# Moving one tile's routing ahead of the last output product in a one-core hybrid decoder layer

## The chip, the core and the metric

One Trainium2 chip, one of its cores, one launch of the kernel. The time is device microseconds (us) from start to end, the median of the runs shown. Below, PE is TensorE, DVE VectorE, ACT ScalarE, POOL GpSimd and SP SyncE, as in the profile.

## The reference

One decoder layer over 256 tokens of width 1024, float32.

```python
h = rmsnorm(x, g_mix)
proj = h @ w_in                      # columns for four token mixers A, B, C, D
b[i] = mixer_i(proj)                 # 256 wide each
merged = sum_i sigmoid(h @ w_gate[i]) * (b[i] @ w_br[i])
x = x + merged @ w_o
h2 = rmsnorm(x, g_ffn)
g_logits = h2 @ w_rg + b_rg          # 4 groups: the largest is taken
e_logits = h2 @ w_re + b_re          # 32 experts, 8 in each group: the two largest of that group
gate = p_group * softmax(the two)
y = sum over the two: gate * ((silu(h2 @ w1[e]) * (h2 @ w3[e])) @ w2[e])
out = rmsnorm(x + y, g_final)
```

## The kernel before

The tokens are two tiles of 128 rows (t = 0, 1), a row of 1024 is two halves of 512 (n = 0, 1). Each engine has a queue of its own, written out by hand in the order of the code; what crosses engines is a semaphore wait. Exact products of float32 weights are made in three PE passes over a high and a low part (`three`).

**The output product.** `out_product(t, n)` computes the quarter (t, n) of merged @ w_o: 8 slices k, three matmuls each, 24 in all. The order of the quarters on PE is (0,0), (1,0), (0,1), (1,1). `turn_tile(1, merged)` stands in the middle of the first; `turn_tile(0, x)`, eight transposes, in the middle of the last. When a quarter is done, DVE adds it to `x` (`add_product`), and `s["wo"]` counts quarters.

**Splitting and turning.** For the experts' gathers each row of x is split in three bf16 parts: `first_part`, `second_part` (ACT), `remain`, `third_part` (DVE), a quarter at a time. For the router the rows of a tile are turned (`turn_tile(t, x)`, PE), weighted by the norm's weights (`weighted_turned`, DVE, into `h2T`) and multiplied by the router's 36 columns (`route(t)` on PE).

**The choices.** When both tiles' router logits are there, DVE makes the choice of group and experts for both tiles at once, a chain in which every instruction waits for the one before (`link`): largest group logit, its one-hot, the mask of the other groups, largest expert, its one-hot, second largest. It ends in `asg`, the assignment. PE counts places from it (five small matmuls, `s["pos"]`), DVE makes `slot` and the one-hot `pick` of the first pair, and PE gathers the rows of the first two experts with `pick` (48 matmuls; L1737). Meanwhile PE puts x into the banks where results are summed (`absorb`) and makes 20 small matmuls whose result is not used (L1720).

**The experts.** 16 pairs of experts. A pair has six matrices of 2 MB (w1, w3, w2 of two experts), each in a unit of a ring of ten. `up` multiplies by w1 and w3 (L1759), `down` by w2 (L1822), `combine` adds to the results. Pair 0 is `experts(0, 0, first=True)`.

**The loads.** SP issues them in one order, each when its unit in the ring has been read. Loads 0 to 5 go to units that the attention part leaves free. Loads 6 and 7 wait for `s["wo"]` to be 2, that is for the second quarter product; loads 8 and 9 go in halves, the first halves when the last product is half done (`s["wo_rows"]`), the second when `s["wo"]` is 4. Loads 10 and 11, the first of the second use of the ring, wait for `s["part_read"]`, which `up` of pair 0 raises after its fourth slice; the rest follow the reads of the pairs:

```python
for units_of, read in (((10, 11), 1), ((12, 13), 2), ((14, 15), 3), ((16, 17), 4)):
    for half in range(2):
        for n in units_of:
            load_half(n, half, read)
```

## Time and profile before

| | us |
|---|---|
| median of 3 runs | 709.2 |
| lowest and highest | 707.84, 709.97 |
| the profiled execution | 708.31 |
| its span | 706.5 |

The span is the stretch in which the profiler saw instructions; 1.8 us of the profiled execution's time lie outside it. PE is busy for 96% of the span, DVE for 35%, ACT for 27%, and the queue of loads moves 344 GB/s on the mean. Times in the rows are counted from the start of the span.

### The profile page before, as it was taken

How to read it: one execution, taken by the hardware profiler on the slowest of the kernel's cores; microseconds unless marked ns; L12 is line 12 of the kernel's file. 1: busy time of each engine (PE TensorE's matmuls, PEld its weight loads, DVE VectorE, ACT ScalarE, POOL GpSimd, SP SyncE). 2: the span in 40 equal slices, each digit the busy share in tenths (PEclk: the TensorE clock that was granted, in tenths of full speed). 3: DMA queues.
4: the chain of work that ended last, by engine and by line, in shares of the span. 5: the costliest groups of instructions: out<-in, count | busy, mean ns of one | idle time of the engine just before them, and what ended most of it. 6: DMA issues, size and time to landing. Idle time of an engine off the chain costs nothing.

```text
span 706.5 us, 9936 instructions
## 1 busy us (share of the span) xinstructions
PE 681.2 (96%) x4047; PEld 398.2 (56%) x4047; DVE 246.4 (35%) x528; ACT 192.7 (27%) x305; POOL 5.2 (1%) x9
## 2 busy tenths in 40 slices
PE   9999999999999999999999999999989898998995
PEld 6999887777777864344344344344344343453433
DVE  7563566667677772121121121121121010210212
ACT  6443565588565421110110010010010010100113
POOL 0000000000000000000000000000000000000000
PEclk9999999999999999999999999999999999999998
DMA  8897741383659959999999999999999999999994
GB/s 311 290 274 232 280 138 54 106 298 119 179 160 384 397 250 376 418 428 426 425 428 427 424 428 426 429 427 426 429 429 428 429 429 424 429 423 428 417 397 169
DMA packets 47053, 243.57 MB, mean 345 GB/s; under 512 B 10352, under 2 KB 13608, under 8 KB 33704
## 3 DMA queue, kind: packets, MB, share of 16 engines
q1 hardware_dynamic: 46568, 241.45, 85.7%
q0 software_dynamic: 448, 1.59, 0.7%
q8 instruction: 27, 0.44, 0.3%
q14 instruction: 10, 0.08, 0.0%
HBM read 241.96 MB, written 1.07 MB: 344 GB/s over the span
## 4 chain that ended last, share of the span: by engine, by line
PE 73%; DMA 17%; DVE 5%; ACT 2%; issue 2%; POOLq 0%; SPq 0%; DVEq 0%; ACTq 0%
PE bank L1759 25%; DMA unit<-in_w 17%; PE bank L1822 10%; PE bank L1434 7%; PE bank L1435 7%; PE bank L1436 7%; PE bank L1737 4%; PE bank L1836 2%; DVE low L340 2%; PE bank L1837 1%; PE bank L1416 1%; PE bank L1796 1%; PE bank L1769 1%; ACT prob L679 1%; PE bank L1661 1%
## 5 line engine op out<-in xcount | busy, mean ns | idle before, releaser
L1759 PE MATMUL bank<-unit,xT 128*64 128x512 f32 x1024 | 229.7, 601 | 11.4 <-DMA unit<-in_w 10.4
L1759 PEld LDWEIGHTS bank<-unit,xT 128*64 128x64 f32 x1024 | 75.8, 138 | 150.2 <-issue 144.5
L1822 PE MATMUL bank<-unit,hidT 128*64 128x512 f32 x480 | 106.3, 595 | 0.0
L1434 PE MATMUL bank<-high,hT_hi 128*128 128x512 f32 (+2 forms) x208 | 79.7, 383 | 1.6 <-DVE low L340 1.1
L1435 PE MATMUL bank<-low,hT_hi 128*128 128x512 f32 (+2 forms) x208 | 77.4, 372 | 0.0
L340 DVE TENSOR_TENSOR low<-unit,high 128x2048 fp32r<-128x2048 f32 (+1 forms) x34 | 70.7, 2098 | 10.3 <-ACT high L335 10.2
L1822 PEld LDWEIGHTS bank<-unit,hidT 128*64 128x64 f32 x480 | 33.1, 137 | 61.5 <-issue 60.0
L1436 PE MATMUL bank<-high,hT_lo 128*128 128x512 f32 (+2 forms) x176 | 65.1, 370 | 0.0
L335 ACT ACTIVATE high<-unit 128x2048 fp32r<-128x2048 f32 (+1 forms) x34 | 59.1, 1758 | 14.6 <-DMA unit<-in_w_in 12.0
L1311 DVE TENSOR_TENSOR y_lo<-bank,y_hi 128x512 fp32r<-128x512 f32 x30 | 20.8, 692 | 94.1 <-ACT y_hi L823 94.1
L1737 PEld LDWEIGHTS bank<-pick,hk 128*128 128x128 bf16 x768 | 44.4, 98 | 13.5 <-issue 12.2
L804 ACT ACTIVATE sg<-bank,slot_rs 128x512 f32<-128x512 f32 x16 | 11.0, 687 | 149.6 <-DVE slot_rs L1274 149.6
L1269 DVE CAST pickT<-bank 128x256 fp32r<-128x256 f32 x15 | 6.4, 425 | 123.7 <-PE bank L1785 123.7
L1737 PE MATMUL bank<-pick,hk 128*128 128x128 bf16 x768 | 48.1, 219 | 0.3 <-DVE pick L1248 0.3
L823 ACT ACTIVATE y_hi<-bank 128x512 fp32r<-128x512 f32 x30 | 17.9, 597 | 106.8 <-PE bank L1822 106.8
L1434 PEld LDWEIGHTS bank<-high,hT_hi 128*128 128x128 f32 x208 | 39.2, 188 | 9.2 <-DVE low L340 2.1
L1295 DVE SCALAR_TENSOR_TENSOR hid<-sg,slot_gate,bank 128x512 f32<-128x512 f32 x15 | 11.2, 748 | 93.8 <-PE bank L1759 93.8
L1435 PEld LDWEIGHTS bank<-low,hT_hi 128*128 128x128 f32 x208 | 39.2, 188 | 6.2
L817 ACT ACTIVATE hidT<-bank 128x512 f32<-128x512 f32 x15 | 9.0, 597 | 115.7 <-PE bank L1769 115.7
L1436 PEld LDWEIGHTS bank<-high,hT_lo 128*128 128x128 f32 x176 | 33.0, 188 | 5.9
L1283 DVE TENSOR_TENSOR xT<-bank,gffn 128x512 f32<-128x512 f32 x32 | 22.1, 692 | 29.3 <-PE bank L1737 29.3
L1836 PE MATMUL bank<-y_hi,pickT 128*128 128x512 f32 x60 | 25.2, 421 | 0.0
(253 smaller groups left out, 681.4 us busy)
## 6 DMA issues: line engine op xcount, KB each, us to landing
unit<-in_w SPq DMA_DIRECT2D x80, 2048.0 KB, 30.4
unit<-in_w SPq DMA_DIRECT2D x24, 1024.0 KB, 10.9
unit<-in_w_gate SPq DMA_DIRECT2D x8, 2048.0 KB, 9.9
unit<-in_w SPq DMA_DIRECT2D x12, 512.0 KB, 15.8
unit<-in_w_in SPq DMA_DIRECT2D x2, 2048.0 KB, 18.0
unit<-in_w_o SPq DMA_DIRECT2D x2, 2048.0 KB, 10.6
unit<-in_w_in SPq DMA_DIRECT2D x6, 512.0 KB, 7.6
unit<-in_w_in SPq DMA_DIRECT2D x3, 1024.0 KB, 12.1
```

What stands on the lines that cost most here:

```text
L335: nc.scalar.activation(hi, w, ACT.Copy).then_inc(s["high"], 1)
L340: ops.tensor_tensor(lo, w, hi.bitcast(F32), ALU.subtract).then_inc(s["low"], 1)
L823: nc.scalar.activation(y_hi[:, n * BANK:(n + 1) * BANK], bank[6 + n][:], ACT.Copy).then_inc(z["yh"], 1)
L1283: V.tensor_tensor(xT[:, 4 * half:4 * half + 4, :], bank[6 + half][:].rearrange("p (k q) -> p k q", k=4), gffn[:, 4 * half:4 * half + 4].un ...
L1311: V.tensor_tensor(y_lo[:, cols], bank[6 + n][:], y_hi[:, cols].bitcast(F32), ALU.subtract).then_inc((z["y0"], z["y1"])[n], 1)
L1434: mm(dst, a_hi, b_hi, start=first, stop=False)
L1435: mm(dst, a_hi, b_lo, start=False, stop=False)
L1436: return mm(dst, a_lo, b_hi, start=False, stop=last)
L1737: last = mm(bank[6 + half][:, c:c + P], part[:, t, k, :], pick[:, t, :], start=(t == 0 and i == 0), stop=(t == NT - 1 and i == 2))
L1759: last = mm(bank[4 + w][g * CAP:(g + 1) * CAP, :], xT[:, k, g * CAP:(g + 1) * CAP], rhs, start=(k == 0), stop=(k == KD - 1))
L1822: last = mm(bank[6 + n][g * CAP:(g + 1) * CAP, :], hidT[:, c, g * CAP:(g + 1) * CAP], rhs[:, c, n * BANK:(n + 1) * BANK], start=(c == 0), ...
L1836: mm(bank[2 * t + n][:], pickT[:, t, :], y_hi[:, cols], start=False, stop=False, skip_group_check=True)
```

## The change

The quarters come in the order (0,0), (0,1), (1,0), (1,1), on PE, DVE and ACT. So tile 0 is complete after two products: its rows are turned in the middle of the third, and its router logits, all eight slices, are computed before the fourth. DVE makes tile 0's choices while PE is in the fourth product. Tile 1 follows alone. The chain of choices is written for one tile, 14 instructions: the mask of groups is folded into one instruction with the help of `group_rank`, and the last comparison writes `asg` itself. The group's `ge` and `oh2` are computed later, behind `picks`, and so is the third part of the last quarter; the first half of the first gather is made in two passes, of which only the second (four matmuls) needs that part. The 20 unused matmuls become 4. `absorb(0, 0)` moves to the place behind the last product. Loads 6 and 7 now wait for `s["wo"]` to be 3. The second half of w_o is split into its low part before `merged_low(1)`. Small tiles are placed elsewhere in SBUF (not shown).

```diff
@@ -72,7 +72,7 @@
-QUARTERS = ((0, 0), (1, 0), (0, 1), (1, 1))
+QUARTERS = ((0, 0), (0, 1), (1, 0), (1, 1))
...
@@ -444,7 +447,7 @@
...
 
-                    sp.wait_ge(s["wo"], 2 + 2 * i)
+                    sp.wait_ge(s["wo"], 3 + i)
 
@@ -452,7 +455,7 @@
-                        sp.wait_ge(s["wo"], 2 + 2 * (k - RING1))
+                        sp.wait_ge(s["wo"], 3 + k - RING1)
@@ -768,32 +771,31 @@
...
-            first_part(0)
-            row_squares(0)
-            first_part(1)
-            row_squares(1)
-            second_part(0)
-            second_part(1)
+            for i in range(2):
+                first_part(i)
+                row_squares(i)
+                if i == 1:
+                    second_norm(0)
+                second_part(i)
+            first_part(2)
             row_squares(2)
-            second_norm(0)
-            first_part(2)
             second_part(2)
             first_part(3)
             row_squares(3)
             second_norm(1)
             second_part(3)
             act.wait_ge(s["eg"], 1)
+            nc.scalar.activation(m[:, 6, :], m[:, 5, :], ACT.Exp).then_inc(s["e2"], 1)
+            act.wait_ge(s["eg"], 2)
...
             merge(3, 3)
-            merged_low(1)
             for half in range(2):
                 low_part(dve, nc.vector, 15, half)
+            merged_low(1)
 
             dve.wait_ge(s["wr"], 16 * 5)
             def add_product(t, n):
-                dve.wait_ge(s["wo"], 2 * n + t + 1)
+                dve.wait_ge(s["wo"], 2 * t + n + 1)
...
+            def route(t):
+
+                one = lambda k: m[:, k, t:t + 1]
+                dve.wait_ge(s["lg_ps"], t + 1)
+                dve.wait_ge(s["rs"], t + 1)
+                link(V.scalar_tensor_tensor(out=lg[:, t, :], in0=bank[4 + t][:, 0:NG + NE], scalar=rs[:, t:t + 1],
+                                            in1=rbias[:], op0=ALU.mult, op1=ALU.add))
+                link(V.tensor_reduce(one(0), lg[:, t, 0:NG], AX, ALU.max))
+                link(V.scalar_tensor_tensor(out=cg[:, t, :], in0=lg[:, t, 0:NG], scalar=one(0), in1=group_rank[:],
+                                            op0=ALU.is_equal, op1=ALU.mult))
+                link(V.tensor_reduce(one(1), cg[:, t, :], AX, ALU.max))
+
+                link(V.scalar_tensor_tensor(out=em[:, t, :].rearrange("p (g e) -> p g e", g=NG),
+                                            in0=cg[:, t, :].unsqueeze(2).broadcast_to([P, NG, EPG]), scalar=one(1),
+                                            in1=lg[:, t, NG:].rearrange("p (g e) -> p g e", g=NG),
+                                            op0=ALU.subtract, op1=ALU.add))
+                for k in (3, 4):
+                    link(V.tensor_reduce(one(k), em[:, t, :], AX, ALU.max))
+                    ranks = ce if k == 3 else oh2
+                    link(V.scalar_tensor_tensor(out=ranks[:, t, :], in0=em[:, t, :], scalar=one(k), in1=iota,
+                                                op0=ALU.is_equal, op1=ALU.mult))
+                    link(V.tensor_reduce(one(k + 4), ranks[:, t, :], AX, ALU.max))
+                    if k == 3:
+                        link(V.tensor_scalar(oh1[:, t, :], ce[:, t, :], one(7), None, ALU.is_equal))
+                        link(V.scalar_tensor_tensor(out=em[:, t, :], in0=oh1[:, t, :], scalar=-NEG, in1=em[:, t, :],
+                                                    op0=ALU.mult, op1=ALU.add))
+                V.scalar_tensor_tensor(out=asg[:, t, :], in0=oh2[:, t, :], scalar=one(8), in1=oh1[:, t, :],
+                                       op0=ALU.is_equal, op1=ALU.add).then_inc(s["asg"], 1)
+
             add_product(0, 0).then_inc(s["x1"], 1)
-            add_product(1, 0).then_inc(s["x1"], 1)
             remain(0)
-            remain(1)
+            squares_so_far(0)
             third_part(0)
-            third_part(1)
+            add_product(0, 1).then_inc(s["x1"], 1)
             link(V.tensor_copy(ident_bf[:], ident))
...
-            add_product(0, 1).then_inc(s["x1"], 1)
+            link(V.tensor_scalar(group_rank[:], iota[:, 0:NG], NEG, None, ALU.mult))
+            remain(1)
             second_norm(0)
-            remain(2)
             weighted_turned(0, 0)
             weighted_turned(0, 1)
+            third_part(1)
+            add_product(1, 0).then_inc(s["x1"], 1)
+            route(0)
+            remain(2)
+            squares_so_far(1)
+            add_product(1, 1).then_inc(s["x1"], 1)
             third_part(2)
-            add_product(1, 1).then_inc(s["x1"], 1)
             weighted_turned(1, 0)
             weighted_turned(1, 1)
             remain(3)
             second_norm(1)
-
-            t4 = lambda ap: ap.unsqueeze(2).broadcast_to([P, NT, NG])
+            route(1)
...
-                link(V.scalar_tensor_tensor(out=lg[:, t, :], in0=bank[4 + t][:, 0:R], scalar=rs[:, t:t + 1],
-                                            in1=rbias[:], op0=ALU.mult, op1=ALU.add))
-            link(V.tensor_reduce(m[:, 0, :], lg[:, :, 0:NG], AX, ALU.max))
-            V.tensor_tensor(ge[:], lg[:, :, 0:NG], t4(m[:, 0, :]), ALU.subtract).then_inc(s["eg"], 1)
...
-                link(V.tensor_reduce(m[:, k, :], em[:], AX, ALU.max))
-                for t in range(NT):
...
-            V.tensor_tensor(asg[:], oh1[:], oh2[:], ALU.add).then_inc(s["asg"], 1)
...
-
-            third_part(3)
             dve.wait_ge(s["pos"], 1)
             link(V.scalar_tensor_tensor(out=slot[:], in0=bank[5][:, 0:NT * NE].rearrange("p (t e) -> p t e", t=NT),
                                         scalar=1.0, in1=asg[:], op0=ALU.add, op1=ALU.mult))
@@ -1322,6 +1326,10 @@
             picks(main, 0, 0, first=True)
+            third_part(3)
+            V.tensor_tensor(ge[:], lg[:, :, 0:NG], m[:, 0, :].unsqueeze(2).broadcast_to([P, NT, NG]),
+                            ALU.subtract).then_inc(s["eg"], 1)
+            link(V.tensor_tensor(oh2[:], asg[:], oh1[:], ALU.subtract))
@@ -1690,43 +1698,57 @@
...
             pe.wait_ge(s["tanh"], 16)
-            out_product(0, 0, range(4))
+            out_product(0, 0)
             pe.wait_ge(s["mrg"], 16)
             turn_tile(1, merged, s["mTps"])
-            out_product(0, 0, range(4, KD))
-            out_product(1, 0)
             out_product(0, 1)
+            out_product(1, 0, range(4))
+            pe.wait_ge(s["x1"], 2)
+            turn_tile(0, x, s["h2ps"])
+            out_product(1, 0, range(4, KD))
+            route(0)
 
             out_product(1, 1, range(4))
-            pe.wait_ge(s["x1"], 3)
-            turn_tile(0, x, s["h2ps"])
             out_product(1, 1, range(4, KD))
-            route(0, range(4))
+            absorb(0, 0)
             pe.wait_ge(s["x1"], 4)
             turn_tile(1, x, s["h2ps"])
-            route(0, range(4, KD))
             route(1)
 
-            def absorb(t, n):
...
             pe.wait_ge(s["bf"], 2)
-            for t, n in ((0, 0), (0, 1), (1, 0)):
+            for t, n in ((0, 1), (1, 0)):
                 absorb(t, n)
-            for _ in range(20):
+            for _ in range(4):
                 mm(bank[7][:, 0:P], ones_bf[:], before_bf[:], start=True, stop=True)
-            pe.wait_ge(s["asg"], 1)
+            pe.wait_ge(s["asg"], NT)
...
-            pe.wait_ge(s["parts3"], 2 * NT)
-
+            pe.wait_ge(s["parts2"], 2 * NT)
+            pe.wait_ge(s["parts3"], 2 * NT - 1)
...
+            def gather_first():
+
+                for with_last in range(2):
+                    for k in range(4):
+                        c = k * P
+                        for t in range(NT):
+                            for i, part in enumerate((hk_1, hk_2, hk_3)):
+                                if (t == NT - 1 and i == 2) == bool(with_last):
+                                    last = mm(bank[6][:, c:c + P], part[:, t, k, :], pick[:, t, :],
+                                              start=(k == t == i == 0), stop=bool(with_last), skip_group_check=True)
+                    if with_last == 0:
+                        pe.wait_ge(s["parts3"], 2 * NT)
+                last.then_inc(main["gat"], 1)
@@ -1894,8 +1916,9 @@
-            for half in range(2):
-                gather(main, 0, half, first=True)
+            pe.wait_ge(main["P"], 1)
+            gather_first()
+            gather(main, 0, 1, first=True)
```

The order of PE's instructions before, from the end of the last product to the counting of places; `wr,h2T` is the router, `x,cst` an absorb, `cst,x` a turning:

```order
L1681 MATMUL bank<-wr,h2T 128x36 x4
L1661 MATMUL bank<-cst,x 128x128 x8
L1681 MATMUL bank<-wr,h2T 128x36 x12
L1713 MATMUL bank<-x,cst 128x512 x3
L1720 MATMUL bank<-before_bf,ones_bf 128x128 x20
L1722 MATMUL bank<-asg,before_bf 128x32
```

Sixteen router matmuls stand behind the last product, in two groups. Now, first the rows where tile 0 is routed (the end of the third product, the router, the start of the fourth):

```order
L1442 MATMUL bank<-high_105,hT_hi 128x512
L1443 MATMUL bank<-low_93,hT_hi 128x512
L1444 MATMUL bank<-high_105,wo_lo 128x512
L1689 MATMUL bank<-wr,h2T 128x36 x8
L1442 MATMUL bank<-high_106,hT_hi 128x512
```

All eight of tile 0's router matmuls now stand ahead of the fourth product. The rows behind the fourth product:

```order
L1703 MATMUL bank<-x,cst 128x512
L1669 MATMUL bank<-cst,x 128x128 x8
L1689 MATMUL bank<-wr,h2T 128x36 x8
L1703 MATMUL bank<-x,cst 128x512 x2
L1728 MATMUL bank<-before_bf,ones_bf 128x128 x4
L1730 MATMUL bank<-asg,before_bf 128x32
```

Eight router matmuls instead of sixteen are left there, and one absorb has moved ahead of the turning.

DVE's rows before, from the end of the chain of choices to the first pick:

```order
L1229 TENSOR_TENSOR oh_155<-ce,m 128x64
L1233 TENSOR_TENSOR asg<-oh_154,oh_155 128x64
L1234 TENSOR_TENSOR m<-m 128x2
L1160 TENSOR_TENSOR hk_129<-remainder_128,hk_63 128x8x64
L1238 SCALAR_TENSOR_TENSOR slot<-bank,asg 128x64
L1240 TENSOR_SCALAR slot<-slot 128x64
L1248 TENSOR_TENSOR pick<-slot,cst 128x256
L1326 TENSOR_REDUCE most<-bank 128x1
```

and now:

```order
L1205 TENSOR_REDUCE m<-oh_152 128x1
L1210 SCALAR_TENSOR_TENSOR asg<-oh_152,m,oh_151 128x32
L1240 TENSOR_TENSOR m<-m 128x2
L1242 SCALAR_TENSOR_TENSOR slot<-bank,asg 128x64
L1244 TENSOR_SCALAR slot<-slot 128x64
L1252 TENSOR_TENSOR pick<-slot,cst 128x256
L1162 TENSOR_TENSOR hk_129<-remainder_128,hk_63 128x8x64
L1330 TENSOR_TENSOR ge<-lg,m 128x8
L1332 TENSOR_TENSOR oh_152<-asg,oh_151 128x64
L1334 TENSOR_REDUCE most<-bank 128x1
```

The third part (L1160 before, L1162 now) has moved from ahead of `slot` to behind `pick`.

## Rows read from the trace of the kernel before

**Rows 1.** Windows: busy time of PE, PEld, DVE, ACT, POOL; clock, DMA share, GB/s.

```profile
236.00:238.00 2.00, 2.00 (x11) 1.59 (x10) 1.77 (x3) 1.66 (x2) 0.00 (x0) 1.00 0.73 262
238.00:258.00 20.00, 18.87 (x119) 14.93 (x117) 14.73 (x44) 8.53 (x17) 0.00 (x0) 1.00 0.98 406
258.00:266.00 8.00, 7.66 (x71) 4.33 (x72) 5.31 (x24) 0.00 (x0) 0.00 (x0) 1.00 0.03 10
266.00:690.00 424.00, 411.91 (x2454) 180.53 (x2452) 70.15 (x189) 41.26 (x66) 0.00 (x0) 0.99 1.01 424
```

**Rows 2.** Chain that ended last, the first load waited for in the pairs: start, us, what.

```profile
497.99 37.89 DMA unit<-in_w
```

**Rows 3.** Timeline of SP: the issues of loads 6, 7 and from 10 on.

```profile
235.61 0.81 SPq L466 DMA_DIRECT2D unit<-in_w  x2
265.16 28.71 SPq L542 DMA_DIRECT2D unit<-in_w  x16
```

**Rows 4.** Chain that ended last, from the last product to the first experts.

```profile
243.98 0.89 PE bank L1661 x8
...
247.67 0.81 PE bank L1681 x8
248.49 1.12 PE bank L1661 x8
249.61 2.62 PE bank L1681 x24
...
261.54 7.02 PE bank L1759 x32
```

**Rows 5.** Timeline of DVE: quarters added, tile 1 turned, the chain of choices, picks.

```profile
227.41 1.29 DVE L1127 SCALAR_TENSOR_TENSOR wo_lo<-bank,hT_hi 128x512 fp32r<-128x512 f32 x2 [2.31 <-ACT hT_hi L750]
228.62 4.48 DVE L340 TENSOR_TENSOR low<-unit,high 128x2048 fp32r<-128x2048 f32 x2
...
241.29 0.69 DVE L1145 TENSOR_TENSOR x<-x,bank 128x512 f32<-128x512 f32 x1 [0.46 <-PE bank L1436]
...
249.20 1.29 DVE L1167 TENSOR_TENSOR h2T<-bank,gffn 128x512 f32<-128x512 f32 x2 [0.80 <-PE bank L1661]
250.40 1.08 DVE L1153 TENSOR_TENSOR remainder<-x,hk 128x512 f32<-128x512 f32 x1
...
252.31 0.26 DVE L1207 SCALAR_TENSOR_TENSOR lg<-bank,rs,rbias 128x36 f32<-128x36 f32 x1 [0.61 <-PE bank L1681]
252.60 0.16 DVE L1209 TENSOR_REDUCE m<-lg 128x2 f32<-128x8 f32 x1
252.80 0.17 DVE L1210 TENSOR_TENSOR ge<-lg,m 128x8 f32<-128x8 f32 x1
...
257.04 0.68 DVE L1160 TENSOR_TENSOR hk<-remainder,hk 128x512 bf16<-128x512 f32 x1
257.65 0.22 DVE L1238 SCALAR_TENSOR_TENSOR slot<-bank,asg 128x64 f32<-128x64 f32 x1
```

**Rows 6.** DVE's groups by form: busy us, mean ns of one.

```profile
L1326 DVE TENSOR_REDUCE most<-bank 128x1 f32<-128x32 f32 x1 | 0.2, 183 | 0.0
```

**Rows 7.** Timeline of PE from the absorbs to the first gathers.

```profile
252.04 2.82 PE L1713 MATMUL bank<-x,cst 128*128 128x512 f32 x6
254.70 1.28 PE L1720 MATMUL bank<-before_bf,ones_bf 128*128 128x128 bf16 x20
257.11 0.19 PE L1722 MATMUL bank<-asg,before_bf 128*128 128x32 bf16 x1 [1.13 <-DVE asg L1233]
...
257.22 0.18 PE L1726 MATMUL bank<-asg,ones_bf 128*128 128x32 bf16 x1
...
258.69 2.84 PE L1737 MATMUL bank<-pick,hk 128*128 128x128 bf16 x48 [0.34 <-DVE pick L1248]
```

**Rows 8.** Timeline of PE, one `up` of a late pair, behind a wait.

```profile
585.05 8.78 PE L1759 MATMUL bank<-unit,xT 128*64 128x512 f32 x32 [2.20 <-DMA unit<-in_w]
```

**Rows 9.** Windows in that `up`, columns as in rows 1.

```profile
586.00:588.00 2.00, 2.00 (x8) 0.82 (x6) 0.00 (x0) 0.00 (x0) 0.00 (x0) 0.50 1.00 426
```

More of the change, by code:

```diff
@@ L248, in hybrid_decoder_layer @@
         cg = place("cg", [P, NT, NG])
+        assert at[0] <= shared + 4 * P
+        pick = place("pick", [P, NT, P], BF16, offset=shared + 4 * P)
+        at[0] = shared + 4 * TOK
         em = place("em", [P, NT, NE])
         ce = place("ce", [P, NT, NE])
+        gate3 = place("gate3", [P, NT, NE, 3], BF16)
+        at[0] = shared + 8 * TOK
         oh1 = place("oh1", [P, NT, NE])
@@ L254, in hybrid_decoder_layer @@
         slot = place("slot", [P, NT, NE])
+        pickT = place("pickT", [P, NT, P], F32R)
+        last_pickT = place("last_pickT", [P, NT, P], F32R)
+        sg = place("sg", [P, DE])
         assert at[0] <= shared + 4 * KD * TOK
@@ L864, in _ @@
                 act.wait_ge(s["squared"], NT + t + 1)
-                act.wait_ge(s["sums"], 3)
+                act.wait_ge(s["sums"], 4)
                 nc.scalar.activation(rs[:, t:t + 1], ss4[:, t, 1:2], ACT.Sqrt, bias=ss[:, t:t + 1],
@@ L1173, in second_norm, with squares_so_far @@
                 V.reciprocal(rs[:, t:t + 1], rs[:, t:t + 1]).then_inc(s["rs"], 1)
+            def squares_so_far(t):
+                dve.wait_ge(s["squared2"], 2 * t + 1)
+                V.tensor_scalar(ss[:, t:t + 1], ss4[:, t, 0:1], 1.0 / D, EPS, ALU.mult, ALU.add).then_inc(s["sums"], 1)
+            iota = cst[:, C_IOTA:C_IOTA + NE]
+            def route(t):
[24 more added lines that the diff above has]
+                                       op0=ALU.is_equal, op1=ALU.add).then_inc(s["asg"], 1)
@@ L1217, in _ @@
-            for t in range(NT):
-                last = V.tensor_tensor(em[:, t, :].rearrange("p (g e) -> p g e", g=NG),
-                                       lg[:, t, NG:].rearrange("p (g e) -> p g e", g=NG),
-                                       ohg[:, t, :].unsqueeze(2).broadcast_to([P, NG, EPG]), ALU.add)
-            link(last)
-            for k, oh in ((3, oh1), (4, oh2)):
-                link(V.tensor_reduce(m[:, k, :], em[:], AX, ALU.max))
-                for t in range(NT):
-                    last = V.scalar_tensor_tensor(out=ce[:, t, :], in0=em[:, t, :], scalar=m[:, k, t:t + 1],
-                                                  in1=cst[:, C_IOTA:C_IOTA + NE], op0=ALU.is_equal, op1=ALU.mult)
-                link(last)
-                link(V.tensor_reduce(m[:, 7, :], ce[:], AX, ALU.max))
-                link(V.tensor_tensor(oh[:], ce[:], t32(m[:, 7, :]), ALU.is_equal))
-                if k == 3:
-                    link(V.scalar_tensor_tensor(out=em[:], in0=oh[:], scalar=-NEG, in1=em[:],
-                                                op0=ALU.mult, op1=ALU.add))
@@ L1714, in absorb @@
                           skip_group_check=True)
+            pe.wait_ge(s["tanh"], 16)
+            out_product(0, 0)
+            pe.wait_ge(s["mrg"], 16)
+            turn_tile(1, merged, s["mTps"])
+            out_product(0, 1)
+            out_product(1, 0, range(4))
[3 more added lines that the diff above has]
+            route(0)
+            out_product(1, 1, range(4))
+            out_product(1, 1, range(4, KD))
+            absorb(0, 0)
+            pe.wait_ge(s["x1"], 4)
+            turn_tile(1, x, s["h2ps"])
+            route(1)
             pe.wait_ge(s["bf"], 2)
-            for t, n in ((0, 0), (0, 1), (1, 0)):
+            for t, n in ((0, 1), (1, 0)):
                 absorb(t, n)
-            for _ in range(20):
+            for _ in range(4):
                 mm(bank[7][:, 0:P], ones_bf[:], before_bf[:], start=True, stop=True)
-            pe.wait_ge(s["asg"], 1)
+            pe.wait_ge(s["asg"], NT)
             mm(bank[5][:, 0:NE], before_bf[:], asg[:, 0, :], start=True, stop=True)
```

35 lines of the change are left out of this document (4 added, 31 removed).

## The prediction

> **What bounds the kernel now.** I looked first at the windows. From 266 to 690 us the DMA engines are busy at a share of 1.01 and move 424 GB/s, while PE has 12 us of idle time; the 8 us before it are nearly empty (share 0.03), and the 20 us before that are full again [rows 1]. The chain of work that ended last confirms the reading: from 498 us on it passes through loads, the first of them 37.89 us long [rows 2]. So from load 10 on the kernel is a stream of weights. 96 matrices less the ten of the ring's first filling are 86 of 2.10 MB, 180 MB; at 424 GB/s that is 425 us, and 266.6 + 425 = 692, which is where the full share ends. The end of the kernel therefore hangs on the moment at which load 10 is issued, 265.16 [rows 3], and this hangs on PE: `up` of pair 0 begins at 261.54 [rows 4] and releases the load 3.6 us later. The window of 1 us behind 266 lies inside the full stretch; I take the data to start 1.4 us after the issue, at 266.6, since 180 MB then end where they are seen to end.
>
> What stands ahead of `up` is a chain over PE and DVE with nothing beside it: last product ready 247.67, turning of tile 1 from 248.49, router until 252.23 [rows 4], choices from 252.31 [rows 5], places at 257.11, gather from 258.69 [rows 7]. Whatever the change saves or adds before 261.54 reaches the end one to one, as long as the loads before load 10 don't get in the way.
>
> **The change, part by part.** Times are of the profiled execution (708.3; the median of the runs is 0.9 higher).
>
> *Router of tile 0 ahead of the last product.* Before, PE had 32 router rows behind the last product (a float32 matmul shows as two), 0.81 + 2.62 = 3.43 us [rows 4]. Sixteen now stand ahead of it: half of that, +1.7. Turning tile 0's x (0.89, rows begin at 243.98 [rows 4]) was ahead of the end before too, now in the third product instead of the fourth: 0 for the end, but +0.9 for the third product. The fourth is ready at 247.67 + 1.7 = 249.4. It has to be said plainly: this step makes PE's path longer, since the router's rows were partly cover for a wait (eight ran while x was added).
>
> *Behind the last product.* Before, it took 252.23 - 247.67 = 4.56 us to the last router row. Now an absorb (2.82 us for three [rows 7], 0.94 each) covers the addition of x (0.69, as at 241.29 [rows 5]), then comes the turning. From the turning's start (248.45 to 248.49) to the end of DVE's second weighting, 249.20 + 1.29 = 250.49 [rows 5], is 2.04; the last eight router rows need 2.62 / 3 = 0.87 after it. With 0.1 of hand-over: 0.98 + 2.04 + 0.05 + 0.87 = 3.95. That is -0.6. The logits of tile 1 are ready at 253.4, 1.1 later than before. DVE's `third_part(2)` (0.68) lies behind the addition and ahead of the first weighting, under the transposes.
>
> *The chain of choices.* Before: 252.31 to PE's first counting matmul at 257.11 [rows 5, 7], 4.80 us for both tiles. Tile 1 alone is 14 linked instructions. The first, 36 columns from PSUM, takes 0.29 start to start, the 8-column ones 0.20 [rows 5]: three of those. The trace has a 32-column reduction of 0.183 [rows 6] and a 64-column operation of 0.22 (`slot` [rows 5]); with the 0.04 between linked instructions (0.20 less 0.16) a 32-column step is 0.22, at most 0.26, at least 0.20. So 0.29 + 3 x 0.20 + 10 x 0.22 + 0.06 = 3.15 (bounds 2.95 and 3.55): -1.65. The broadcast operand of the folded mask is not in the trace as a scalar_tensor_tensor; I price it as the others. Choices for tile 0 are another 3.1 us of DVE, from about 243.8 to 246.9; they lie under the fourth product. Behind them come `remain(2)` (1.08 [rows 5]) and one small one, until 248.2, and the addition of the fourth quarter is due at 249.5: 1.3 us of slack, and when it is used up everything behind the last product moves. `remain(3)`, once done 0.8 before the chain, now ends at about 253.5 with the reciprocal behind it, when the logits come at 253.4: up to 0.2 late. I count 0.1.
>
> *Third part behind the picks.* `slot` started at 257.65, 0.25 after the counting ended (257.22 + 0.18), because the third part held DVE from 257.04 [rows 5, 7]. Now it starts at once: -0.2. The third part then lies under the first 20 matmuls of the gather, 20/48 of 2.84 = 1.18 us [rows 7], and needs 0.68; the gather stays 2.84. Were it late, four matmuls would wait for at most 0.5.
>
> *Low part of w_o before `merged_low(1)`.* DVE was idle for 2.31 us until 227.41, that is from 225.1, ahead of `merged_low(1)`; the two instructions of 4.48 us [rows 5] now start there and end at 229.6. Half a product takes 247.67 - 243.98 - 0.89 = 2.80 [rows 4]; three products and a turning back from 241.25, the first started at 223.5, so the second now starts at 223.5 + 5.6 + 0.9 = 230.0 and finds both. `merged_low(1)` (1.29) is needed for the third at 235.6. 0.
>
> *16 matmuls less.* 20 took 1.28 [rows 7] and ended 1.13 before the assignment came. The two absorbs left and four of these end at about 255.5, the assignment comes at 256.6: the same idle 1.1. 0, with a rival below. Moving `ge`, `oh2` behind the picks: two of 0.2 ahead of the first `xT`, which has 0.9 of gather to hide in. 0.
>
> Sum on PE: +1.7 - 0.6 - 1.65 + 0.1 - 0.2 = **-0.65**. `up` of pair 0 starts at about 260.9, load 10 is issued at 264.5.
>
> *Loads 6 and 7.* They were issued at 235.61 [rows 3], and the queue was just running dry (share 0.73 in the two microseconds from 236 [rows 1]). Now they wait for the third product, 241.25 + 0.89 = 242.1: the DMA engines lose 6.5 us there. Loads 6 to 9 are 8.4 MB, at the 406 GB/s of that stretch 20.7 us; starting 1.4 after the issue they end at 264.2. Load 10's data would start at 264.5 + 1.4 = 265.9. So the new hole is taken from the old one of 8 us and costs nothing, by a margin of 1.7 us. It also is a ceiling: no gain on PE beyond 266.6 - 264.2 = 2.4 us can reach the end.
>
> 708.3 - 0.65 = 707.7; against the median 709.2 that is **708.5**.
>
> **A rule against the trace.** The gap of 1.13 us on PE before the counting was no harm: the gather behind it ran 48 matmuls in 2.84 us [rows 7]. A gap of 2.20 us at 585 was harm: the granted clock stood at 0.50 of full, 1.2 GHz, from 586 to 588 [rows 9], and the `up` took 8.78 [rows 8] instead of 7.02 [rows 4]. The Trainium skill, page "TensorE: Matmul & The Clock Gate", section "Part 1: The HAM clock gate", says that the clock of the matrix engine falls to half when the engine has been idle and comes back after sustained work, independently of what the kernel intends; it speaks against taking 16 filling matmuls away. By the rule the sum could be 1.8 us worse; by the row of the 1.13 us gap it is as I have it.
>
> **Rivals.**
> 1. *The clock falls* (slower). If the gap before the counting grows towards 2.2 us, as it does if the chain starts late, the gather and first `up` run at half clock: 8.78 - 7.02 = +1.76, all of it ahead of load 10. 708.5 + 1.8 = 710.3. It decides somewhere between a gap of 1.13 and one of 2.20; I expect 1.1. Chance 0.10.
> 2. *The loads become the bound ahead of load 10* (slower). If the third product comes at 244 or later, or four loads take more than 22.4 us, the hole at 237 to 243 is no longer paid by the old one, and PE's start doesn't matter. With 3 us late: about 710.5. Against it: PE was busy for 2.00 of 2.00 us in the second product's stretch [rows 1], so the products wait for nothing, and what they need of x stands 1.5 us ahead. Chance 0.05.
> 3. *DVE's slack of 1.3 us is used up*: the fourth addition is late, the gain is gone: 709.2. Chance 0.15.
> 4. *The steps are at their low bounds and waits I kept vanish*: -1.2 to the ceiling of -2.4: 706.8 to 708. Chance 0.15.
> 5. The forecast, -0.65 with -1.1 to -0.2 around it: 0.55.
>
> **How the numbers follow.** The runs before spread over 2.1 us, 0.3%, which is also about what a measurement can tell from no change. Only the far end of rival 4 passes the bound below, only rivals 1 and 2 with a run on the high side pass it above: faster 0.07, same 0.85, slower 0.08. The range, from 709.2 - 2.4 = 706.8 to rival 1 at 710.3: 706.8 to 710.3.
>
> **What the profile after would show.** The fourth product ending near 249.4; the logits of tile 1 near 253.4 and the assignment near 256.6; `up` of pair 0 at 260.9 and load 10 issued at 264.5; a hole in the DMA share from 237.5 to 243.5 and a shorter one before 266; then the same 424 GB/s to an end 0.65 earlier. I am wrong if load 10 is issued and its data start doesn't follow it, if the third product comes behind 243, if the granted clock falls in 255 to 262, or if the choices of tile 0 end behind 249.

## The result and the profile after

The changed kernel took 710.62 us in the median of 20 runs (709.52 to 712.5), the kernel before, on the same chip, 709.12 us in 20 runs (707.84 to 710.05): ratio 1.0025, 95% interval 1.0018 to 1.0031. Forecast were 708.5 and a range to 710.3, so the time lies above the range, on the other side of "before". The profiled execution has a span of 709.3 us, against 706.5.

The windows of the changed kernel, in the places of [rows 1] (columns as there):

```profile
236.00:238.00 2.00, 2.00 (x10) 1.62 (x9) 1.55 (x4) 0.64 (x2) 0.00 (x0) 1.00 0.80 328
238.00:242.00 4.00, 4.00 (x23) 3.40 (x22) 3.30 (x8) 2.52 (x5) 0.00 (x0) 1.00 0.03 10
242.00:244.00 2.00, 2.00 (x15) 1.78 (x14) 0.81 (x2) 0.11 (x1) 0.00 (x0) 1.00 0.00 0
244.00:264.00 20.00, 18.01 (x129) 12.94 (x130) 14.87 (x52) 6.73 (x12) 0.00 (x0) 1.00 1.00 405
264.00:268.00 4.00, 4.00 (x20) 1.29 (x18) 2.95 (x15) 0.00 (x0) 0.00 (x0) 1.00 0.45 127
268.00:690.00 422.00, 408.67 (x2440) 177.87 (x2436) 68.92 (x186) 40.63 (x64) 0.00 (x0) 0.99 1.01 424
```

The loads behave as forecast. The old hole of 8 us ahead of load 10 is now one of 6 us at 238 to 244, where loads 6 and 7 wait, and one of some 3 us ahead of 267; then comes the same 424 GB/s. The timeline of SP has the issues, load 10's at 266.14:

```profile
243.16 0.80 SPq L469 DMA_DIRECT2D unit<-in_w  x2
...
266.14 28.96 SPq L545 DMA_DIRECT2D unit<-in_w  x16
```

The timeline of PE and that of DVE between the last product and the first gather, where [rows 4, 5, 7] have the kernel before:

```profile
250.34 1.02 PE L1703 MATMUL bank<-x,cst 128*128 128x512 f32 x2
251.28 1.16 PE L1669 MATMUL bank<-cst,x 128*128 128x128 f32 x8
252.78 1.98 PE L1689 MATMUL bank<-wr,h2T 128*128 128x36 f32 x16 [0.34 <-DVE h2T L1169]
254.59 1.96 PE L1703 MATMUL bank<-x,cst 128*128 128x512 f32 x4
256.39 0.39 PE L1728 MATMUL bank<-before_bf,ones_bf 128*128 128x128 bf16 x4
258.29 0.19 PE L1730 MATMUL bank<-asg,before_bf 128*128 128x32 bf16 x1 [1.51 <-DVE asg L1210]
...
259.67 1.50 PE L1747 MATMUL bank<-pick,hk 128*128 128x128 bf16 x24
261.01 1.50 PE L1759 MATMUL bank<-pick,hk 128*128 128x128 bf16 x24
```

```profile
248.06 0.25 DVE L1210 SCALAR_TENSOR_TENSOR asg<-oh,m,oh 128x32 bf16<-128x32 f32 x1
248.23 1.21 DVE L1155 TENSOR_TENSOR remainder<-x,hk 128x512 f32<-128x512 f32 x1
249.36 0.14 DVE L1180 TENSOR_SCALAR ss<-ss 128x1 f32<-128x1 f32 x1
250.54 0.69 DVE L1147 TENSOR_TENSOR x<-x,bank 128x512 f32<-128x512 f32 x1 [1.04 <-PE bank L1444]
...
254.24 0.15 DVE L1175 RECIPROCAL rs<-rs 128x1 f32<-128x1 f32 x1
254.79 0.26 DVE L1189 SCALAR_TENSOR_TENSOR lg<-bank,rs,rbias 128x36 f32<-128x36 f32 x1 [0.41 <-PE bank L1689]
...
256.24 0.25 DVE L1203 SCALAR_TENSOR_TENSOR ce<-em,m,cst 128x32 f32<-128x32 f32 x1
256.52 0.19 DVE L1205 TENSOR_REDUCE m<-ce 128x1 f32<-128x32 f32 x1
256.74 0.24 DVE L1207 TENSOR_SCALAR oh<-ce,m 128x32 f32<-128x32 f32 x1
257.02 0.19 DVE L1208 SCALAR_TENSOR_TENSOR em<-oh,em 128x32 f32<-128x32 f32 x1
```

The tile 0 choices end at 248.3, and the fourth addition still starts 0.2 after the last product: DVE's slack held. `up` of pair 0 begins at 262.44 in the timeline, in the kernel before at 261.46. But this whole execution was already 1.03 us later when tile 0 of `merged` was turned (222.14 against 221.11): the granted clock stood at 0.50 from 151 to 154, long ahead of any edit. A repeat of the same kernel (e4 below) was at 221.35 there; e3, the kernel before with later loads, has such a fall there too and was at 222.81. From that turning to `up` it takes 40.30 us, before 40.35. So the edits on the path that was costed bring **-0.05**, and none of them loses anything.

The loss is elsewhere. The page of the changed kernel, with the line that differs (the kernel before has 27 packets and 0.44 MB):

```profile
span 709.3 us, 9914 instructions
q8 instruction: 36, 0.59, 0.3%
L1781 PE MATMUL bank<-unit,xT 128*64 128x512 f32 x1024 | 229.6, 600 | 12.8 <-issue 6.3
```

and PE's timeline where its loop over the experts starts the second pass (pair 7), changed kernel first, then the kernel before:

```profile
438.57 7.09 PE L1844 MATMUL bank<-unit,hidT 128*64 128x512 f32 x32
448.47 1.97 PE L1781 MATMUL bank<-unit,xT 128*64 128x512 f32 x4 [2.81 <-issue]
453.94 8.27 PE L1781 MATMUL bank<-unit,xT 128*64 128x512 f32 x28 [3.50 <-issue]
```

```profile
437.59 7.09 PE L1822 MATMUL bank<-unit,hidT 128*64 128x512 f32 x32
444.51 7.04 PE L1759 MATMUL bank<-unit,xT 128*64 128x512 f32 x32
```

(Pairs 2 to 11 are a loop of five pairs in PE's program, run twice; pair 7 opens the second pass.) PE stands still for 6.3 us in which it waits for nothing that a semaphore shows ("issue"). What happens then is in queue q8, which brings PE's instructions in packets of 16 KB: the kernel before fetches none between 434.6 and 598.8 us, the changed kernel eight between 445.3 and 557.7 and a ninth at 581.1. From the start of `up` to the end of the span it takes 446.81 us, before 445.06: **+1.75**. With -0.05 that is 1.7; the medians differ by 1.5.

### The profile page after: what moved, and what is told of

It reads as the page before. It is cut to its first block, busy times and chain, and to the rows that moved or that the text cites. A ratio compares the mean times of both kernels' runs of the same rounds, so it can differ in the third digit from the quotient of the medians.

```text
span 709.3 us, 9914 instructions
## 1 busy us (share of the span) xinstructions
PE 681.5 (96%) x4031; PEld 397.4 (56%) x4031; DVE 248.0 (35%) x538; ACT 192.7 (27%) x305; POOL 5.2 (1%) x9
## 4 chain that ended last, share of the span: by engine, by line
PE 76%; DMA 12%; DVE 5%; issue 3%; ACT 2%; SPq 1%; POOLq 0%; DVEq 0%; ACTq 0%
PE bank L1781 26%; DMA unit<-in_w 12%; PE bank L1844 12%; PE bank L1442 7%; PE bank L1443 7%; PE bank L1444 7%; PE bank L1759 5%; PE bank L1858 2%; DVE low L343 2%; PE bank L1859 1%; SPq L568 1%; PE bank L1424 1%; PE bank L1791 1%; ACT prob L682 1%; PE bank L1487 1%
```

## The experiments

Loop distance is the stretch from the start of `up` of pair 0 to the span's end, from each run's own trace. "Packets" are PE's instruction packets (those of GpSimd behind the plus). "Issue" is PE's idle time of that sort ahead of the second pass. "Last load" is the end of the last load, counted from the issue of load 10 and taken from the traces' records of DMA packets. A filler is one of the small matmuls whose result is not used. Each kernel was timed against the kernel before, in 4 to 12 executions of its own, whose medians in the four batches were 708.62 (e1 to e4), 708.97 (e5 to e8), 708.96 (e9 to e11) and 708.57 (e12 to e15).

| run | packets | issue, us | loop distance | last load | median | ratio, 95% interval |
|---|---|---|---|---|---|---|
| before | 27 | none | 445.1 | 430.2 | | |
| changed kernel | 36 | 6.3 | 446.8 | 431.9 | 710.62 | 1.0025 [1.0018, 1.0031] |
| e4, changed kernel again | 36 | 7.2 | 446.9 | 432.0 | 710.72 | 1.0027 [1.0015, 1.0038] |
| e1, changed, 20 fillers | 27 | none | 444.9 | 430.1 | 709.15 | 1.0003 [0.9994, 1.0012] |
| e2, before, 4 fillers | 36 | 5.8 | 447.0 | 432.1 | 712.04 | 1.0041 [1.0027, 1.0056] |
| e3, before, late loads | 27 | none | 444.9 | 430.1 | 708.93 | 1.0 [0.9991, 1.0009] |
| e5, changed, 16 matmuls early | 27 | none | 445.6 | 430.7 | 709.71 | 1.0011 [1.0, 1.0021] |
| e6, changed, 20 fillers, 16 warming less | 36 | 6.2 | 446.8 | 431.9 | 712.5 | 1.0041 [1.0026, 1.0056] |
| e7, changed, 12 fillers | 27 | none | 445.1 | 430.2 | 708.79 | 0.9997 [0.9988, 1.0006] |
| e8, changed, 20 fillers, 16 early | 28 | none | 447.4 | 430.2 | 712.01 | 1.0038 [1.0024, 1.0052] |
| e9, before, nine copies | 27 | none | 446.4 | 431.5 | 709.86 | 1.0012 [1.0003, 1.0021] |
| e10, before, one copy | 27 | none | 445.6 | 430.7 | 709.09 | 1.0004 [0.9995, 1.0013] |
| e11, before, stall on both passes | 27 | none | 448.1 | 433.2 | 712.28 | 1.0048 [1.0034, 1.0062] |
| e12, before, GpSimd fetches | 27 + 18 | none | 453.9 | 439.1 | 717.99 | 1.0131 [1.0116, 1.0147] |
| e13, before, GpSimd fetches twice that | 27 + 36 | none | 465.8 | 451.0 | 729.06 | 1.0283 [1.0268, 1.0297] |
| e14, before, one late stall | 27 | none | 445.0 | 430.2 | 709.37 | 1.0007 [0.9997, 1.0016] |
| e15, control for e14 | 27 | none | 445.0 | 430.1 | 708.86 | 1.0 [0.999, 1.0009] |

**Which edit it is.** e1 gives the changed kernel its 20 filling matmuls back, e2 takes 16 out of the kernel before, e3 gives the kernel before the later loads alone.

```
-            for _ in range(4):       (e1; e2 is the reverse)
+            for _ in range(20):
                 mm(bank[7][:, 0:P], ones_bf[:], before_bf[:], start=True, stop=True)

-                    sp.wait_ge(s["wo"], 2 + 2 * i)      (e3, and likewise for load 7)
+                    sp.wait_ge(s["wo"], 3 + i)
```

> The changed kernel with the 20 unused matmuls of before in place of the 4. Theory A (the idle gap of 1.51 us on PE ahead of the counting, against 1.13 before, lets the granted clock fall in part of the executions, which costs up to 1.76 us each time): the gap shrinks to about 0.5 us and the median falls from 710.6 to 709.1 to 709.8, the high half of the runs goes. Theory B (the later issue of loads 6 and 7 costs the time): no change, 710.6. Theory C (neither; something of the whole program, such as its layout or the spread of the load engines): no change, 710.6.

> The kernel before with only the 4 fillers of the change, nothing else. Its PE gap ahead of the counting grows from 1.13 to about 2.1 us. Theory A: slower than 709.1, by 0.5 to 1.8, with a wider spread. Theories B and C: 709.1 as before.

> The kernel before, in which loads 6 and 7 wait for the third quarter product (5.6 us later), nothing else. Theory B: slower by 1 to 2 us although load 10 is issued at the same time as before, because the queue, once emptied, fills the units in another rhythm. Theories A and C, and the sum of the prediction: 709.1, the new hole in the loads is taken from the old one.

> The changed kernel once more, for a second trace: 710.6. The first trace has a fall of the granted clock at 151 to 155 us, in a part of the program that the change doesn't touch, and starts the output product 1.0 us later than before. If that is chance, this trace starts it within 0.5 us of the kernel before (turning of tile 0 at 221.1). The stretch from that turning to the issue of load 10 should again be within 0.2 us of before's 44.05; if it is, the loss of 1.5 us is not made in the stretch that the change edits but behind it, in the weight stream or the tail (theory C).

The number of fillers alone moves the kernel between the two groups of the table, from either side; the late loads do nothing (in e3 load 10 is issued 3.7 us behind the start of `up`, as before, and the last load ends at its old distance). But it isn't the clock in the gap. In e2 the gap grew to 2.02 us, and the counting and the gather behind it ran at a granted clock of 1.00; in the changed kernel the clock is 1.00 there too. The loss appears 190 us further on.

**Gap or place.** Sixteen fillers are 32 of the 7117 instructions that PE's program has with 20 of them (a weight load and a matmul each). Counted in PE's compiled program, the loop body is instructions 3827 to 5493 with 20 fillers and 3795 to 5461 with four. e5 keeps the gap and restores the place; e6 closes the gap and keeps the wrong place; e7 and e8 try two more places.

```
                     pe.wait_ge(s["small"], 16 * 9)      (e5; e8 too, with range(20) fillers)
+                    for _ in range(16):
+                        mm(bank[7][:, 0:P], ones_bf[:], ones_bf[:], start=True, stop=True)

-            keep_warm(23)                               (e6, with range(20) fillers)
+            keep_warm(7)
```

> The changed kernel with its four filling matmuls, and 16 matmuls into bank 7, whose result nobody reads, put far ahead, in the projections before the bias table (some 1 us of PE there). PE's idle gap before the counting stays near 1.5 us; the expert loop stands in PE's instruction stream where it stood before the change. Theory P (place of the loop in the stream): no issue stall at the start of the loop's second pass, 27 instruction packets, from up of pair 0 to the end of the span 445.0, and about 709. Theory G (the longer gap, or the fewer matmuls in it, do the harm in some other way): stall of 6 us, 36 packets, 446.9, and 710.7.

> The changed kernel with 20 filling matmuls in the gap, but 16 of the 23 warming matmuls at the very start left out, so that the expert loop stands where it stands in the changed kernel. Gap near 0.6. Theory P: the issue stall of some 6 us comes back, 36 packets, 446.9 from up of pair 0 to the end. Theory G: no stall, 27 packets, 445.0. The start of the kernel may itself be slower or faster for lack of warming, so the stretch behind up decides, not the time.

> The changed kernel with 12 filling matmuls: the loop stands 16 instructions later than in the changed kernel, and 16 earlier than in the kernel before. Theory P says only that it is one or the other or between: 27 or 36 packets, with 445.0 or 446.9 behind up, or a part of the stall with fewer packets. Theory G: gap near 1.0, less than before had, so no stall, 709.1.

> The changed kernel with 20 filling matmuls and the 16 early ones as well: the loop stands 32 instructions later in PE's stream than in the kernel before. Theory P: if what matters is that the loop stands late enough, 27 packets or fewer and 445.0 behind up, about 709 to 710 (the early matmuls cost up to 1 us); if it depends on where the loop lies between the pieces of 16 KB, it can be worse or better. Theory G: as with 20 fillers, 445.0 and 27 packets.

PE's timelines of e5 and of e6 (its gap first) decide it:

```profile
259.46 0.19 PE L1732 MATMUL bank<-asg,before_bf 128*128 128x32 bf16 x1 [1.51 <-DVE asg L1210]
...
446.66 7.04 PE L1783 MATMUL bank<-unit,xT 128*64 128x512 f32 x32
```

```profile
260.41 0.19 PE L1730 MATMUL bank<-asg,before_bf 128*128 128x32 bf16 x1 [0.62 <-DVE asg L1210]
...
450.53 1.98 PE L1781 MATMUL bank<-unit,xT 128*64 128x512 f32 x4 [2.75 <-issue]
455.97 8.32 PE L1781 MATMUL bank<-unit,xT 128*64 128x512 f32 x28 [3.46 <-issue]
```

With the gap of 1.51 us and the old place there is no stall; with a gap of only 0.62 and the new place it is back. The place decides. A shift of 16 instructions from the old one (e7) is harmless, one of 32 (the change) is not. e5 is 0.6 us longer behind `up` than the others of its group (its last load ends at 430.7), which I can't explain; the rest of what its traced execution lost lies ahead of `up`. e8 is a surprise: no stall at the second pass, yet 447.4. There the work ends where it should (the output is stored from 703.24 on, in the kernel before from 701.84; `up` was 1.36 later too) and its last load ends at 430.2 like the others', but the span goes on for 4.7 us behind the end of the stores instead of 2.5, and a 28th packet is recorded there, at 705.62. So the closing instructions of PE can be what is fetched late as well; I take this from one trace, and no run tested it.

**By which way 1.8 us.** PE's stall of 6 us is more than the loss. Either it reaches the end in part, or it is absorbed and the packets do it in the DMA engines, which the kernel is bound by. In the changed kernel the DMA share stays at 1.01 right through the stall (first row; the clock ahead of it is 0.50). The other rows are windows of its last microseconds; the second fence has those of the kernel before:

```profile
449.00:457.00 8.00, 4.50 (x12) 1.00 (x10) 0.00 (x0) 0.00 (x0) 0.00 (x0) 0.50 1.01 424
...
693.00:694.00 1.00, 1.00 (x8) 0.37 (x6) 0.00 (x0) 0.00 (x0) 0.00 (x0) 1.00 0.78 289
694.00:695.00 1.00, 1.00 (x8) 0.23 (x4) 0.00 (x0) 0.00 (x0) 0.00 (x0) 1.00 0.63 223
695.00:696.00 1.00, 0.48 (x4) 0.09 (x4) 0.00 (x0) 0.49 (x1) 0.00 (x0) 1.00 0.52 195
696.00:697.00 1.00, 1.00 (x10) 0.69 (x12) 0.69 (x1) 0.10 (x1) 0.00 (x0) 1.00 0.48 170
697.00:698.00 1.00, 1.00 (x9) 0.50 (x6) 0.00 (x0) 0.00 (x0) 0.00 (x0) 1.00 0.30 111
```

```profile
692.00:693.00 1.00, 1.00 (x8) 0.15 (x4) 0.00 (x0) 0.00 (x0) 0.00 (x0) 1.00 0.78 291
693.00:694.00 1.00, 1.00 (x10) 0.59 (x10) 0.00 (x0) 0.57 (x1) 0.00 (x0) 1.00 0.64 238
694.00:695.00 1.00, 1.00 (x12) 0.47 (x8) 0.69 (x1) 0.03 (x1) 0.00 (x0) 1.00 0.43 160
695.00:696.00 1.00, 1.00 (x6) 0.67 (x4) 0.00 (x0) 0.00 (x0) 0.00 (x0) 1.00 0.09 31
```

Both begin to run out at 0.78, one microsecond apart, which is the shift of load 10 (266.14 - 265.16). Then half of the engines of the changed kernel have work for two microseconds more (0.52, 0.48, 0.30), and PE waits 0.52 us for the last piece, where before it didn't wait. Six experiments tried this: traffic of the same size in other forms, a stall without fetches, fetches without a stall.

```
+            for k in range(9):                          (e9, ahead of SP's loop)
+                sp.dma_start(dram_copy[k], <16 KB in a row of w_o>).then_inc(s["extra"], 16)

+            sp.dma_start(dram_copy, a["w_o"][0, 0:P, 0:288]).then_inc(s["extra"], 16)     (e10)

+                if late:                                (e11: first pair of each pass; e14: pair 7)
+                    dve.wait_ge(main["B"], p + 1)
+                    V.tensor_reduce(ge[:], cst[:, 0:800] (8 times over), AX, ALU.max)
                 hidden(main, p, first, last)

+            for _ in range(9 * 512):                    (e12, on GpSimd; e13: 18 * 512)
+                pool.wait_ge(s["pos"], 1)
```

> The kernel before, and nine copies of 16 KB each from memory to memory, one contiguous row apiece, issued by SP just ahead of its loop of loads (about 1/16 of a pair's weights in all, and no change for any engine but SP). PE has no stall here. Theory D (what the changed kernel loses comes through the DMA engines: nine packets of 16 KB and 1.1 us each hold up a few of the 16 engines, and the last load lands with the slowest of them): later by about 1 to 2 us if the copies gather on a few engines, by 0.3 to 0.7 if they spread evenly. Theory S (PE's stall of 6 us at the loop's second pass does it): as before, 708.9, or later by no more than the bytes, 0.35.

> The kernel before, and the same 147 KB copied in one transfer of 128 rows, issued at the same place. Theory D: the bytes spread over the engines, so that no more than about 0.35 to 0.7 us is lost, clearly less than in the changed kernel. Theory S: the same, no difference beyond the bytes.

> The kernel before, and on DVE one reduction of 6400 elements, some 6.7 us, ahead of the hidden product of the first pair of each pass of the expert loop (pairs 2 and 7), whose result nobody reads. PE waits some 5 to 6 us for it in both passes; the number of instruction packets stays 27. Theory D: the stream of loads goes on beneath (share 1.01) and PE catches up: from up of pair 0 to the end stays near 445.0, 709, at most 0.5 later. Theory S: the stall reaches the end, 1.9 us or more later, 711 and above. A stall at pair 2, when the ring has only just been filled again, may cost something on its own; then a hole in the DMA share behind it would show that.

> The kernel before, and on GpSimd, which is idle there, 2304 waits (instructions of 64 B, 147 KB, nine pieces of 16 KB) on a semaphore that has long been reached, behind the counting. Only the fetching of them should touch the rest; PE has no stall. If they come in packets like PE's (36 in all or so): theory D 446.3 to 447 from up of pair 0 to the end, and about 710.5; theory S 445.0 and 709. If no packets are recorded for them, the run tells nothing.

> The same with 4608 waits, 18 pieces. Theory D: about twice the loss of the nine, 448 to 449 and 712; theory S: 445.0 and 709.

> The kernel before with DVE's loop over the pairs written out straight, and the reduction of 6.7 us ahead of pair 7's hidden product alone, so that PE stalls some 6 us once, at the place where it stalls in the changed kernel, with nothing fetched. Theory D: absorbed, within 0.5 us of the same kernel without the reduction. Theory S: 1.9 us later than it.

> The control: DVE's loop written out straight, without the reduction. Both theories: as before, 445.0 behind up and about 709.

e9's copies were cut into 288 small packets and e10's into 144, so they don't show what nine packets of 16 KB do; they cost 1.3 and some 0.6 us behind `up`, more than the 0.35 us that 147 KB take at 424 GB/s, and more in e9's form. e11 is no clean test either: its first stall, at pair 2, opened a hole in the loads. Windows of e11:

```profile
340.00:350.00 10.00, 10.00 (x55) 4.41 (x55) 1.38 (x2) 1.32 (x3) 0.00 (x0) 0.87 0.82 345
350.00:370.00 20.00, 20.00 (x132) 9.35 (x130) 3.87 (x11) 1.28 (x2) 0.00 (x0) 1.00 0.99 405
...
460.00:480.00 20.00, 13.87 (x86) 6.86 (x83) 9.00 (x9) 0.78 (x2) 0.00 (x0) 0.89 1.00 427
```

The hole is 10 x (1.01 - 0.82) + 20 x (1.01 - 0.99) = 2.3 of the 3.0 us that e11 lost; the rest is open. The stall at pair 7 leaves no hole. e14 has it alone (DVE's loop over the pairs is written out straight there, as in its control e15). PE's timeline of e14:

```profile
468.74 1.13 PE L1772 MATMUL bank<-cst,hid 128*128 128x128 f32 x4 [6.13 <-DVE hid L1295]
...
595.26 7.09 PE L1762 MATMUL bank<-unit,xT 128*64 128x512 f32 x32 [0.24 <-DMA unit<-in_w]
```

and the loop distance is 445.0, that of its control. PE makes the 6 us up by waiting less for loads: its first wait for one is at 595, in the control at 526. The stall begins at 462.6, some 17 us later than in the changed kernel (445.7), and is absorbed; the changed kernel itself shows no hole behind its stall. The medians differ by 0.5 us, with intervals that overlap.

e12 and e13 are the other half. Of the 4608 and 9216 waits written, on a semaphore that has long been reached, the compiled program keeps 2304 and 4608. No engine's work is touched, and the page counts the fetches of GpSimd as the queue q14, in packets of 8 KB; e12's line and then e13's (the kernel before has 10, 0.08):

```profile
q14 instruction: 28, 0.23, 0.1%
```

```profile
q14 instruction: 46, 0.38, 0.1%
```

The same 147 KB as PE's nine packets cost 8.9 us behind `up`, twice that 20.8: 0.49 and 0.58 us for each packet of 8 KB. Evenly spread, 147 KB would be 0.35 us. Windows of e12 show where the rest is:

```profile
266.00:675.00 409.00, 392.21 (x2350) 174.54 (x2348) 67.33 (x180) 37.27 (x59) 0.00 (x0) 0.99 1.01 424
675.00:695.00 20.00, 19.73 (x94) 6.90 (x92) 2.08 (x8) 3.37 (x5) 0.00 (x0) 1.00 0.84 298
695.00:699.00 4.00, 3.36 (x18) 1.80 (x16) 0.87 (x2) 0.77 (x2) 0.00 (x0) 1.00 0.99 369
```

The rate is untouched until 675, and in the 20 us behind it part of the engines is out of work while the loads still aren't complete. My reading is that one engine, or a few, did the fetching and is behind: each load is spread over all 16 and lands with the last of them. How the fetches are spread, no record names. That fetches without a stall cost the end, and a stall without fetches doesn't, is shown.

The records of the load packets show the same for PE's nine. Counted from the issue of load 10:

| | 75 MB | 120 MB | 175 MB | last load |
|---|---|---|---|---|
| before | 179.2 | 284.3 | 413.6 | 430.2 |
| e14, stall, no fetch | 179.0 | 284.3 | 413.5 | 430.2 |
| changed kernel | 179.0 | 284.9 | 414.4 | 431.9 |
| e2, before, 4 fillers | 179.1 | 284.9 | 414.3 | 432.1 |

75 MB is where the first of the nine is fetched (445.2 us). From there to 120 MB the two kernels that fetch lose some 0.6 us of the stream, 0.8 us until 175 MB, and the last 6 MB bring it to 1.7 to 1.9. The kernel with the stall alone loses nothing. So the loss comes through the loads, with the fetches. Spread evenly, the bytes would cost 0.35. The durations of the nine packets (1.02 to 1.10 us) repeat with a period of eight, as they would if eight engines took turns; nine packets over eight engines would be 1.2 us for each, an estimate that leaves some 0.5 open.

**A version that beats both?** e7 is the changed kernel at a good place: 708.79 us, 0.9997 [0.9988, 1.0006]. It undoes the loss and gains nothing that can be measured, as -0.05 on the path says. It is the best of these, and no better than the kernel before.

## Why the prediction was wrong

Its sum, term by term, us on PE's path (measured from the same rows in both traces):

| term | forecast | measured | from |
|---|---|---|---|
| router rows of tile 0 ahead of the last product | +1.7 | +1.64 | turning of `merged` to product: 26.56, now 28.20 |
| behind the last product, to the first choice | -0.6 | -0.19 | 4.64, now 4.45 |
| chain of choices | -1.65 | -1.30 | 4.80, now 3.50 |
| `remain(3)` | +0.1 | 0 | reciprocal ends 254.39, logits at 254.79 |
| third part behind the picks | -0.2 | -0.20 | 1.58, now 1.38 |
| late loads 6 and 7 | 0 | 0 | e3 |
| 16 matmuls less | 0 | +1.75 to +1.9 | both traces, e1, e2, e6 (by e5 1.2) |
| sum | -0.65 | +1.7 to +1.85 | |

**The step that failed** is "*16 matmuls less.* ... the same idle 1.1. 0, with a rival below". The idle time was priced, and rightly (1.51 us without harm). What wasn't seen is that a matmul taken away also moves every instruction behind it: the expert loop starts 32 instructions earlier in PE's stream, and at that place its second pass is fetched from memory again, nine packets of 16 KB, into a kernel that is bound by the DMA engines. Rival 1 named the right edit with the wrong mechanism, and that its size (+1.76) is the measured one is a coincidence. Its condition, half clock in the gather, didn't come about; the granted clock was 1.00 there. It does fall to 0.50 in the stall, from 449 to 457, where PE had stood still, and there it is absorbed with the stall. The Trainium skill, page "TensorE: Matmul & The Clock Gate", section "Part 1: The HAM clock gate", says that the clock falls to half when the engine has been idle. The trace agrees at the stall, and shows no fall at the shorter gap of 1.51 us, nor does e2's at 2.02. None of my signs of error in the last paragraph of the prediction was one of this kind: I watched nothing behind load 10, because the path was handed over to the loads there.

**Two terms were mis-sized**, together by 0.76 us. Behind the last product I let only eight router rows come after DVE's second weighting. The router of tile 1 has 16, they can't start before the first half of `h2T` (252.78), and at 1.98 us they are longer than that half's remainder: the rows themselves are the bound, and the eight that once ran ahead of them as cover were given away. In the chain, an operation whose scalar operand is a column just written takes 0.24 to 0.25 us on 32 columns, a reduction 0.19; I priced both by the reduction of 0.183 [rows 6]. From start to start that is 0.28 in five places where I had 0.22, and 0.25 for `cg` where I had 0.20, together the 0.35; 3.50 lies inside my upper bound of 3.55. One reading was wrong and changed nothing: the window 236 to 238 in [rows 1], by which rival 2 calls PE busy in the second product, lies in the third, since the second was ready at 235.61.

**What was right**: the late loads. The new hole was taken out of the old one, with the predicted third product (243.13 against 242.1 plus this execution's 1.03) and no cost. So was the bound: what reached `up` reached load 10, and load 10 the end, one to one, plus what the packets took. On the path that was costed, what the edits save and what they cost nearly cancel (-0.05); the forecast gain of 0.65 was not there.

## What to carry to other kernels

Where a kernel is bound by its loads, whatever else goes through the DMA engines counts, the fetching of instructions included, and it can cost much more than its bytes (147 KB, worth 0.35 us at the stream's rate, cost 1.8 us here and 8.9 us in e12): compare the count of instruction packets of both profiles before looking at anything else. An edit to straight code ahead of a long loop can change it by moving the loop, so look for idle time named "issue" at the loop's back edge, and try the edit again with some instructions more or fewer ahead of the loop before judging it. A filler matmul that warms nothing may be holding a loop in its place. Where the loop is long, count in the compiled program how many packets its body touches.

## What the runs showed of the hardware

- A loop body of 1667 PE instructions is kept for its second pass where it lies in seven packets of 16 KB (started at instruction 3811, 3825, 3827 or 3859 of the program) and fetched anew where it lies in eight (3795, 36 packets instead of 27, in all three kernels that had it there), with 5.8 to 7.2 us of stall. That the number of packets decides is inferred from these five places.
- GpSimd fetched 147 KB of instructions while it did nothing but wait, and the kernel became 1.3% slower; 295 KB made it 2.8%.
- The span can go on for 2.3 us longer with the work ended at its usual distance, and one more instruction packet at the end (e8).
- DVE, 32 columns of float32: 0.19 us for a reduction or with a constant as scalar, 0.24 to 0.25 with a column as scalar operand.
- Six us of idle PE late in a stream of loads cost nothing (e14: last load at 430.2 us behind load 10, as without), while nine fetched packets moved that end by 1.7 to 1.9 us.
